# Scatter of returned rows issued ahead of the gather and of the weight loads in GpSimd's round

## The reference

```python
def _moe(h, l, w_router, b_router, w_e_gate, w_e_up, w_e_down, ...):
    s = sigmoid(t @ w_router)                       # 64 scores a token
    _, sel = top_k(s + b_router, 8)
    g = take_along_axis(s, sel); g = g / sum(g) * 2.5
    ...
    for each group of experts:
        hid = silu(t @ w_e_gate) * (t @ w_e_up) * gates      # 128 wide
        out = out + hid @ w_e_down
```

## Time and profile before

| what | before |
|---|---|
| time, median of 3 runs | 1328.1 us (1319.62 to 1328.82) |
| the profiled execution | 1333.55 us, span 1331.8 us, mean granted TensorE clock 0.961 |
| PE busy | 1201.4 us, 90% of the span |
| POOL busy | 383.5 us, 29% |
| chain that ended last | PE 73%, DMA 11%, DVE 5%, issue 3% |
| DMA queue of SP (q1) | 178.32 MB |
| software DMA queue of GpSimd (q0) | 79.66 MB |

### The profile page before, as it was taken

The page is one execution under the profiler, slowest core; times in us unless marked ns, Lnnn a source line. Parts: engine busy times, 40 slices in busy tenths (PEclk is TensorE's granted clock), DMA queues, the critical chain, the costliest instruction groups (busy, mean ns, idle before and its releaser), DMA issues.

```text
span 1331.8 us, 26951 instructions
## 1 busy us (share of the span) xinstructions
PE 1201.4 (90%) x10827; PEld 709.1 (53%) x10827; DVE 550.1 (41%) x1348; ACT 392.3 (29%) x953; POOL 383.5 (29%) x447
## 2 busy tenths in 40 slices
PE   3699997999989898899779999999999999999786
PEld 1498895667754555444345554455555455545332
DVE  2607891233256477245736533232332222222235
ACT  2324432233345477111212222222222222222201
POOL 2043333423310232001023343343443333434200
PEclk7799998999989899899889999999999999999989
DMA  7322226544270000402539987977877778786297
GB/s 299 127 84 73 90 81 213 179 145 152 74 270 1 1 1 1 151 32 78 230 123 370 345 299 274 342 276 277 324 284 294 260 283 321 277 300 221 76 407 231
DMA packets 61738, 262.05 MB, mean 197 GB/s; under 512 B 24190, under 2 KB 24270, under 8 KB 47662
## 3 DMA queue, kind: packets, MB, share of 16 engines
q1 hardware_dynamic: 27072, 178.32, 36.4%
q0 software_dynamic: 33968, 79.66, 16.8%
q10 hardware_dynamic: 576, 2.36, 0.5%
HBM read 297.81 MB, written 53.69 MB: 264 GB/s over the span
## 4 chain that ended last, share of the span: by engine, by line
PE 73%; DMA 11%; DVE 5%; issue 3%; ACT 2%; POOL 2%; SPq 0%; POOLq 0%; DVEq 0%; ACTq 0%
PE bank L1812 20%; PE bank L1833 11%; PE bank L1796 6%; PE bank L1667 5%; DMA x_got<-x_dram,idx_tok 5%; PE bank L1377 4%; PE bank L1379 4%; DMA pairs<-pair_dram 4%; PE bank L1378 4%; PE bank L1486 3%; PE bank L1562 2%; PE bank L1406 2%; PE bank L1818 1%; PE bank L1606 1%; DMA w_stage<-in_w_ada 1%
## 5 line engine op out<-in xcount | busy, mean ns | idle before, releaser
L1812 PE MATMUL bank<-slot,xt 128*32 128x256 f32 x5376 | 310.2, 383 | 11.3 <-issue 8.6
L1812 PEld LDWEIGHTS bank<-slot,xt 128*32 128x32 f32 x5376 | 170.8, 110 | 121.4 <-issue 15.6
L1833 PE MATMUL bank<-slot,hid_t 128*32 128x512 f32 x1344 | 161.6, 598 | 0.4 <-ACT hid_t L1344 0.4
L1040 POOL DMA_INDIRECT pair_dram<-out_rows,idx_pair x84 | 86.0, 1024 | 217.3 <-DVE out_rows L2302 193.6
L1377 PE MATMUL bank<-h_hi,w_hi 128*128 128x288 f32 x480 | 145.2, 302 | 1.1 <-DVE h_lo L1949 1.1
L1378 PE MATMUL bank<-h_lo,w_hi 128*128 128x288 f32 x480 | 141.4, 295 | 0.0
L1379 PE MATMUL bank<-h_hi,w_lo 128*128 128x288 f32 x480 | 141.3, 294 | 0.0
L2302 DVE COPY out_rows<-bank 128x512 f32<-128x512 f32 x84 | 58.1, 691 | 146.5 <-PE bank L1833 76.6
L2296 DVE TENSOR_TENSOR hid<-sg,bank 128x128 f32<-128x128 f32 x84 | 24.1, 287 | 214.2 <-ACT sg L1338 213.9
L652 POOL TENSOR_TENSOR w_lo<-w_stage,w_hi 128x1024 fp32r<-128x1024 f32 x29 | 69.4, 2392 | 129.2 <-ACT w_hi L1089 99.7
L1023 POOL DMA_INDIRECT x_got<-x_dram,idx_tok x84 | 85.5, 1018 | 72.3 <-DVE idx_tok L2280 43.2
(11 more groups left out here) (335 smaller groups left out, 1562.4 us busy)
## 6 DMA issues: line engine op xcount, KB each, us to landing
slot<-in_w_moe SPq DMA_DIRECT2D x65, 1536.0 KB, 9.7
w_stage<-in_w_ada SPq DMA_DIRECT2D x32, 512.0 KB, 4.6
pairs<-pair_dram SPq DMA_DIRECT2D x16, 1024.0 KB, 9.9
w_stage<-in_w_in SPq DMA_DIRECT2D x30, 512.0 KB, 3.5
resid<-in_w_ada SPq DMA_DIRECT2D x2, 2048.0 KB, 11.3
feat<-in_w_ada SPq DMA_DIRECT2D x2, 2048.0 KB, 12.7
w_out_sb<-in_w_out SPq DMA_DIRECT2D x1, 4096.0 KB, 14.7
o_t<-in_x_t ACTq DMA_DIRECT2D x4, 576.0 KB, 14.2
```

Source lines behind the costliest of these rows:

```text
L1040: g.indirect_dma_start(pair_dram, bass.IndirectOffsetOnAxis(ap=idx_pair[:, j, c:c + 1], axis=0), out_rows[:, i % 2, :], None, bounds_check ...
L1812: ins = mm(bank[2 + i % 2][r, 0:2 * P], xt[:, i % 2, k, r], slot_of(load)[:, 2 * P * k:2 * P * (k + 1)], start=(k == 0), stop=(k == KD - 1 ...
L1833: ins = mm(bank[4 + 2 * (i % 2) + c][r, :], hid_t[:, i % 2, r], slot_of(load)[:, 2 * D + 512 * c:2 * D + 512 * c + 512], start=True, stop= ...
```

## The change

In each round the scatter of the step just finished is issued first, ahead of the gather and of the late units' weight loads; before it came last. Nothing else is changed: the number of issues, their waits and their sizes are the same.

```diff
             for i in range(1, N_STEPS + 1):
+                scatter(i - 1)
                 if i + 3 < N_STEPS:
                     gather(i + 3)
                 for load in range(6 + 1, N_UNITS + 1):
                     if is_over(load) and last_step_of(load - 6) == i - 1:
                         load_over(load)
-                scatter(i - 1)
```

## The result

The changed kernel takes **1375.5 us** (median of four runs, 1371.0 to 1384.2) against 1327.6 us of the kernel before on the same chip: a ratio of 1.037, 95% interval 1.032 to 1.042, or 48 us more. The forecast was 1356, in a range of 1334 to 1400: the sign was right and the time lies in the range, but some 20 us of it were not foreseen at their place.

What follows compares the result with a forecast made beforehand. The prediction took TensorE's nearly closed chain in the expert loop as the bound, with weight loads on their deadline. Load 18, clock 5 and gather 5 summed to 28 us on 1328: 1356 us, 2.1% slower, range 1334 to 1400.

Steps and rivals of the forecast that it cites:

- What bounds the loop: Expert loop: TensorE's chain is nearly closed, so any reordering can win at most about 10 us, 0.8%.
- The scatter's gain at nothing: Scatter issued earlier in rounds with a load: ScalarE's 80.6 us of waits are hidden, gain nothing, at most 1.2 us.
- The load: GpSimd's 22 weight loads, issued 3.4 us later behind scatter and gather: 18 us of TensorE stalls (9 to 42).
- The shift of 2.0 us: How much later GpSimd's load lands: about the middle of 1.2 and 3, the scatter's and gather's own transfer time.
- SP's next load in front: Rival: engines alternate between queues, SP's next load cuts into GpSimd's late one, shift 4.5 us, time 1416; chance 0.17.
- The gather: Gather loses one step of lead: 5 us (3 to 9) in the loop's first dozen steps, nothing later.
- My third rival: Early stretch dominates: 7 steps late by 2 to 3 us, some 18 us, 1374; chance inside the forecast's 0.65.
- The clock: TensorE's granted clock falls after stalls of about 3 us, 1.34 us each: 5 us (0 to 10).
- Not slower: Rival: SP's load hides the later issue, GpSimd's load is no later in effect, shift under 0.5 us, 1328 to 1331; chance 0.15.
- What would show it: Signs in the new profile: weight waits some 27 us, load issue at 6.1 us, shorter landings, ScalarE's scatter waits falling.
- The last sign of being wrong: TensorE waiting for gathers in every round, which would mean the 7.6 us lead was the undercosted term.

Runs made afterwards that it cites:

- the best one found: Kernel before with round load, gather(i+4), scatter(i-1), gather one step deeper, and SP's next load held until the late unit's weights have landed: 1318.1 us, ratio 0.994.
- The fifth kernel: Kernel before with round load, gather(i+4), scatter(i-1): load first, gather one step deeper, scatter last: 1322.5 us, ratio 0.996.
- the third experiment: Changed order with the gather one step deeper: scatter(i-1), gather(i+4), load: 1354.1 us, ratio 1.020 against the kernel before.
- the first experiment: Kernel before with only the load moved, behind the scatter: gather(i+3), scatter(i-1), load: 1334.4 us, ratio 1.005.
- The seventh: Kernel before with the gather one step deeper and the load held until the next expert products are through, nothing new ahead of it: 1353.5 us, ratio 1.017.
- the ninth: Changed order with gather one step deeper, plus SP's next load held until the late unit's weights have landed: 1336.6 us, ratio 1.009 against the kernel before.
- sixth: Changed order in rounds 1 to 8 only, the kernel before's order from round 9 on: 1341.9 us, ratio 1.011 against the kernel before.
- eighth: Kernel before's order in rounds 1 to 8, changed order from round 9 on: 1365.1 us, ratio 1.026 against the kernel before.
- The second experiment: Kernel before with the gather moved last: load, scatter(i-1), gather(i+3): 1487.5 us, ratio 1.122.
- fourth: Kernel before's order with the gather one step deeper: gather(i+4), load, scatter(i-1): 1326.3 us, ratio 0.999.

## Why the prediction came out as it did

**What bounds the loop: right.** TensorE's waits, of about 10 us, were the most that an order could win, and the best one found won 8.

**The scatter's gain at nothing: right.** The 80.6 us of ScalarE's waits vanished and no time came back. The fifth kernel is the proof from the other side: in it ScalarE waits more for scatters than before (113.4 us), and it is faster.

**The load: the size right, the mechanism half wrong.** 18 us of stalls and 5 of clock were forecast for it; the third experiment has 19.9 and 5.2 in its profile and 26 in its time. The shift of 2.0 us is 1.8 in the changed kernel and 2.3 in the third (16.30 and 16.81 against 14.51). The sum over the single landings also holds at a second point: the text gives 12.1 us in fourteen for a shift of 1.2, against 6.4 for none, which for 22 loads is 9; the first experiment has a shift of 1.16, in its one profile, and cost 6. But the shift does not come from where I took it, the transfer time of a scatter and a gather beside SP's tail. The seventh has nothing new ahead of its load and the same shift; the ninth gets 1.5 of 2.3 us back by keeping SP's next load away. That the later issue is largely hidden was right for the load's start: 1 us is left of 3.45. The rest of the 2.3 us arises on the way to the landing, and 1.5 us go when SP's next load is kept away. The 2.0 of the forecast was the middle of two bounds for another cause; that it met the measured shift is in part luck.

**SP's next load in front** was my second rival, at 1416. Its mechanism is shown, its size is not: the shift was 2 us, not 4.5. The Trainium skill's rule, page "DMA: Bandwidth & Descriptors", section "Queues, rings and completion order", by which an engine goes round the queues a packet at a time, goes with the two loads that slow each other in the third experiment; it does not make SP's load pass, which was issued 2.5 us behind and landed 1.5 us behind. The packets in these traces name their queue and not their engine, so their order on one engine is not shown.

**The gather: the step that was mis-sized.** It stands in the prediction as 5 us early and, later in the loop, "enough unless SP's load overlaps; I cost that at nothing". Measured: 14 us early (sixth) and about 11 later (eighth less third), 25 in place of 5, with their share of the clock. Early, I looked at steps 6 and 7, found delays of 2 to 3 us, and stopped. In the sixth step 6 waits 6.9 us and step 9 another 5.6; in the changed kernel steps 5 and 6 wait 2.8 together and step 9 waits 5.42, after a gather that took 13. My third rival had 18 us for this stretch and came nearest (1374 in all), though as seven short waits where there are two long ones, and without the later gathers; that its sum nearly meets the measured time is luck. I had argued it down by the demand that falls when TensorE is held up. Later, I had a lead of 7.6 us and no landing to set against it, and I asked about SP's load where GpSimd's own is the one ahead: in every third step the gather stands behind the last round's load in the queue and takes up to 10.1 us. The second experiment, with a load directly ahead, shows how that goes on.

The trace of the kernel before held the warning. For the turn of step 6 I took the landing of the scatter of 706.74 as the earliest that the gather behind it could land, and allowed little more. That gather, issued at 708.05, landed only at 722.0 by the last count of the semaphore that tells of it, 6.3 us too late for the turn at 715.70; the sixth waited 6.9 there. From issue to landing the gathers before take 8.6 us on the mean of steps 12 to 79, and those of every third step from 13 to 76 take 11.5 to 15.2, with a lead of 7.6 + 6.7 = 14.3. The 1.2 us of waits for gathers in the earlier trace rows fall on four of these steps (13, 22, 25 and 67): the lead was already used up there.

That the time lies in the range is owed to the room left for a dearer load. The gather's own bounds, 3 to 9 us, were too narrow.

**The clock:** 5 us were forecast, for stalls of 3 us and more at the loads; that is what the third experiment shows (5.2). In the changed kernel TensorE's busy time in the loop grew by 11.1, and its longest wait for weights was 2.6 us. In windows of 50 us the granted clock is 0.90 from 700 to 750 and 0.96 from 750 to 800, 0.97 in three later ones and 1.00 in the rest: the largest loss lies in the early stretch, after the gathers' long waits, which the term did not hold.

**Not slower**, the first rival, fell: it needs a shift under 0.5 us. **What would show it** held for the load's issue, for ScalarE's waits and for the shorter landings counted from the issue (11.7 to 10.0 us on the mean, 1.7 less; 1.4 forecast). It missed for the waits ahead of L1812, 18.0 where some 27 were said: with TensorE also held up by gathers, some loads are on time again. The third, without these, has 28.5. The last sign of being wrong came half true: TensorE waits for gathers not in every round but in every third, and the lead of 7.6 us was indeed the term that I undercosted.

What stays open: why the fifth's loads land 1.24 us sooner than the fourth's with the same issue time; and how much of the hold's 1.5 us a load in the old order would also gain, since that order was not run with the hold (the early loads of the fifth gained 0.3).

## What to carry to other kernels

Where several transfers are issued from one queue, write down for each its lead, from issue to use, and how long it takes at worst in its place in the queue (not a typical one), and go through every one of a full stretch: a moved wait costs at each item that stood behind it. A wait that lies under another engine's work, however long (80 us here), is no reason to reorder; look whether the bounding engine waits for it. If a buffer is free a step before the written order uses it, ask for the data a step earlier, put what is wanted soonest first and what waits longest last, and keep the next bulk transfer of another queue away until the urgent one has landed.

## What the hardware showed

Issuing a 1.5 MB load 3.9 us later cost 2.3 us of landing with nothing new ahead of it in its own queue (seventh against fourth). In the third experiment, 3.45 us later, its first packet moved only 1 us later and the landing came 2.3 us later; 1.5 of these came back when another queue's load of the same size, issued 2.5 us behind it, was held. Kept apart, two such loads took 9.0 and 7.5 us on the mean; together 10.6 and 10.9. A gather behind such a load took 11.5 to 15.2 us in the kernel before, 8.6 on the mean of all. After one wait of 5.42 us the next 6.9 us ran at a granted clock of 0.51, which made it cost half as much again.
